# All ten key and value tiles of a transformer block summed by quarters, the context loaded and multiplied ahead of q, and the w_ada chunks in another order

## The chip, the cores and the metric

The kernel is one layer of a diffusion transformer on the 8 cores of one Trainium2 chip. The program is the same on each core, and no core talks to another: a core takes 1,024 of the 8,192 tokens (two samples of 4,096), a halo of 128 tokens on either side for the windowed keys, and its sample's 256 context tokens. The metric is the device time of the slowest core, in microseconds (us). Each core has a matrix engine (TensorE, PE in the profile), a vector engine (VectorE, DVE), ScalarE (ACT), GpSimd (POOL, used here only to issue loads) and SyncE (SP, issues the small loads, x and the stores).

## What is computed

```
m      = silu(c) @ w_ada + b_ada              # 6 x 2048 per sample: shift, scale, gate (mixer), shift, scale, gate (MLP)
h      = x * (1 + scale) + shift              # m[0], m[1]; the context has its own m from c_ctx
q,k,v,u,g = split(h @ w_in)                   # 1024, 256, 256, 1024, 1024 columns
k_ctx, v_ctx = (h_ctx @ w_in)[:, 1024:1536]
attn   = softmax over 384 window keys (axial rope on q, k), 256 context keys and a sink; 8 q heads, 2 kv heads
gmlp   = gelu(u) * (w_s @ LN(gelu(g)) + b_s)  # chunks of 128 positions
x      = LN(ALPHA * x + gate * ([attn, gmlp] @ w_out))
x      = LN(ALPHA * x + gate2 * (relu((x * (1 + scale2) + shift2) @ w_ff1) ** 2 @ w_ff2))
```

## The kernel before

The program is written as one list of operations. `P.add` notes what each reads and writes, and puts it at the end of its engine's list; a wait is set for each overlap with an earlier operation of another engine. So every engine runs its operations strictly in the order in which the code names them, and the code's order is the schedule. Loads stand in the list of POOL (weights, xT, context, rope tables, masks) or of SP (bias rows, x_tm, LayerNorm rows), and the list waits at a load whose target isn't free yet. Weights come in slots W0 to W3 of 16 KB per partition; `wload` takes the slot whose last use is the earliest, and loads 2,048 KB (bf16, read as 4 MB of fp32). PSUM has 8 banks, `PSB[0]` to `PSB[7]` (`psd` in the profile is 0 to 3, `ps` is 4 to 7); `bank()` takes the next of the list that `use_banks` has set.

The stages that the change touches:

- Start (L487 to L602). w_ada (2048 x 12288) is used in 24 chunks of 512 columns; chunk n of `ada_chunk` (L434) is 16 matmuls, a copy to `MT` (L449), and at the next `ada_flush` either four tiny matmuls and an addition into a column table `MODCOL` (chunks 0 to 7 and 12 to 19; L417, L423) or, for a gate (chunks 8 to 11, 20 to 23), one matmul and an addition into `GATE` (L409, L412). Chunks 0 to 7 are shift and scale of the mixer, and h needs them. For each quarter q of the 2,048 rows, four tiles of xT are loaded into `XTR`, chunks 4+q and q are computed, four tiles `HT` of h are formed (ACT even, VectorE odd), and key/value tiles 0 to 5 (128 tokens by 512 columns) are advanced by 4 matmuls each in banks 0 to 5 (L483). Tiles 6 to 9 are done whole behind it, 16 matmuls each (`kv_mm`, L340). `kv_evac` applies rope to k (four VectorE operations, L467 to L475) and copies v (L534); `kv_tr` transposes k. The context is loaded into `CTXT` over `XTR6` and `XTR7`, so only after the last tiles of h; 16 ACT operations form `HCT`, and `ctx_k`, `ctx_v` multiply it. Between them stand two tiles of q with the weight `Wq0`, and `bb_half`, which adds the row sums of w_s to the bias `BB` (L589).
- Attention loop (L685 to L770). 32 steps of scores, exp, transposes and products with v are laid beside 14 groups of q (steps with `qphase`), 16 of u and the first of g. `q_ada` and `u_ada` name the steps that carry a w_ada chunk.
- g stage and output projection (L834 to L945). 16 groups of g; `g_mix(t)` is the gating product of tile t (L799) with its VectorE chain (L804, L808); `g_ada` names the groups behind which a chunk stands. Then `wout_group(W, n, t)`: 16 matmuls, three VectorE operations (L824, L825, L814), the second of which needs tile t of x from `x_tm`. The x tiles 0 to 4 lie over `HT` and are loaded when the last g group is done. The groups of n = 0 stand in the order t = 5, 0, 6, 1, 7, 2, 3, 4.

Behind that come LayerNorm, the MLP in four passes and the last LayerNorm, which take 920 us and which the change leaves as they are.

## Time and profile before

| | |
|---|---|
| median of 3 runs | 1521.34 us (1520.41 to 1590.14) |
| profiled execution | 1515.89 us |
| its span, slowest core (core 4) | 1514.3 us |
| spans of the 8 cores | 1502.5 to 1514.3 us |
| TensorE busy | 1356.9 us, 90% |
| VectorE, ScalarE, GpSimd busy | 666.4, 341.8, 50.2 us |
| mean granted clock of TensorE | 0.961 |
| moved by DMA | 179.93 MB, 119 GB/s over the span |

Times in rows are microseconds from the start of the span of core 4, unless marked ns. The granted clock is a share of 2.4 GHz; 0.5 is 1.2 GHz. A row of the timeline is a run of like instructions of one engine: start, duration, and, in brackets, how long the engine had been idle and what it waited for.

### The profile page before, as it was taken

The page shows a single profiled execution, that of the slowest core. Times are in us where ns is not written, and L with a number is a line of the kernel's source. Part 1 is how long each engine was busy: PE and PEld are TensorE (multiplying, and loading weights), DVE is VectorE, ACT ScalarE, POOL GpSimd, SP SyncE. Part 2 cuts the span into 40 slices and gives each one's busy share as a digit, 9 for nine tenths or more (in the row PEclk, how much of TensorE's full clock was granted, in tenths as well). Part 3 has the DMA queues.
Part 4 walks back from the last instruction along what each step waited for, and adds up shares of the span by engine and source line. Part 5 has one row for each costly group of instructions (what it writes and reads, how often), then busy time and mean ns, then how long its engine had stood idle before and what let it go on. Part 6 is the DMA issues. An engine that isn't in the chain of part 4 may idle for free.

```text
span 1514.3 us, 19786 instructions; the slowest of 8 cores (1502.5 to 1514.3 us)
## 1 busy us (share of the span) xinstructions
PE 1356.9 (90%) x7289; PEld 660.1 (44%) x7430; DVE 666.4 (44%) x1215; ACT 341.8 (23%) x603; POOL 50.2 (3%) x94
## 2 busy tenths in 40 slices
PE   0343889999898999999999999999999999999995
PEld 0121455566444444444444444444444444444442
DVE  0010567788577567662344222443222333112677
ACT  0000256656553005521000111000111000111232
POOL 2010100000000000000000000000000000000000
PEclk9855899999999999999999999999999999999998
DMA  9999998667668994489542432523424425339312
GB/s 180 202 200 204 212 167 146 111 119 133 126 133 161 247 163 84 98 139 173 99 90 56 90 78 56 111 57 70 98 56 84 83 56 104 63 64 157 115 77 91
DMA packets 22687, 179.93 MB, mean 119 GB/s; under 512 B 3200, under 2 KB 7552, under 8 KB 11968
## 3 DMA queue, kind: packets, MB, share of 16 engines
q0 software_dynamic: 15328, 155.42, 55.8%
q1 hardware_dynamic: 7264, 23.23, 4.4%
q8 instruction: 61, 1.00, 0.3%
q14 instruction: 34, 0.28, 0.1%
HBM read 311.26 MB, written 8.39 MB: 211 GB/s over the span
## 4 chain that ended last, share of the span: by engine, by line
PE 75%; DMA 12%; DVE 4%; issue 4%; ACT 3%; another core or an unknown queue 2%; POOL 0%; DVEq 0%; ACTq 0%; SPq 0%; POOLq 0%
PE psd L340 31%; PE ps L340 30%; PE ps L483 6%; DMA regW<-w_in 3%; DMA regW<-w_ada 3%; DMA regW<-w_ff 2%; DMA regA<-x_tm 2%; PE ps L348 2%; DMA regB<-ctxT 2%; ACT regD L329 1%; PE ps L443 1%; DVE regD L625 1%; PE ps L666 1%; ACT regC L329 1%
## 5 line engine op out<-in xcount | busy, mean ns | idle before, releaser
L340 PE MATMUL ps<-regC,regW 128*128 128x512 bf16 (+1 forms) x1048 | 234.4, 378 | 6.0 <-ACT regC L329 3.3
L340 PE MATMUL psd<-regC,regW 128*128 128x512 bf16 x1052 | 237.0, 379 | 1.0
L329 ACT ACTIVATE regD<-ps 128x512 f32<-128x512 f32 (+1 forms) x91 | 57.0, 626 | 521.3 <-PE ps L340 511.4
L340 PEld LDWEIGHTS ps<-regC,regW 128*128 128x128 bf16 x1072 | 104.7, 98 | 130.6 <-issue 8.4
L340 PEld LDWEIGHTS psd<-regC,regW 128*128 128x128 bf16 x1072 | 104.6, 98 | 127.6 <-issue 1.6
L969 DVE TENSOR_TENSOR regW<-regD 128x512 bf16<-128x512 f32 x64 | 44.3, 693 | 179.7 <-ACT regD L329 179.7
L340 PE MATMUL ps<-regW 128*128 128x512 bf16 x504 | 120.2, 379 | 0.4
L340 PE MATMUL ps<-regW,regB 128*128 128x512 bf16 x502 | 120.1, 379 | 0.5
L340 PE MATMUL psd<-regW,regB 128*128 128x512 bf16 x439 | 104.9, 379 | 2.1 <-DMA regW<-w_ff 1.6
L340 PE MATMUL psd<-regW 128*128 128x512 bf16 x437 | 104.8, 379 | 0.6
L969 DVE TENSOR_TENSOR regB<-regD 128x512 bf16<-128x512 f32 x48 | 33.2, 693 | 132.5 <-ACT regD L329 132.5
L981 DVE TENSOR_TENSOR regD<-psd,regD 128x512 f32<-128x512 f32 x64 | 44.2, 691 | 103.7 <-PE psd L340 103.7
L981 DVE TENSOR_TENSOR regD<-ps,regD 128x512 f32<-128x512 f32 x64 | 44.2, 690 | 101.8 <-PE ps L340 101.8
L443 PE MATMUL ps<-regW,regC 128*32 128x512 bf16 x128 | 14.9, 616 | 81.9 <-DMA regW<-w_ada 81.9
L483 PE MATMUL ps<-regW,regA 128*128 128x512 bf16 x319 | 78.9, 388 | 1.0 <-issue 0.2
L329 ACT ACTIVATE regD<-psd 128x512 f32<-128x512 f32 x63 | 37.6, 597 | 175.3 <-PE psd L340 175.3
L340 PEld LDWEIGHTS ps<-regW,regB 128*128 128x128 bf16 x512 | 50.0, 98 | 60.5
L340 PEld LDWEIGHTS ps<-regW 128*128 128x128 bf16 x512 | 50.0, 98 | 60.5
L986 DVE TENSOR_TENSOR regA<-regA,regD 128x512 f32<-128x512 f32 x96 | 66.5, 692 | 10.0
L340 PEld LDWEIGHTS psd<-regW,regB 128*128 128x128 bf16 x448 | 43.7, 98 | 54.8 <-issue 2.1
L340 PEld LDWEIGHTS psd<-regW 128*128 128x128 bf16 x448 | 43.7, 98 | 53.0
L340 PE MATMUL psd<-regW,regC 128*128 128x512 bf16 x281 | 64.9, 385 | 0.4
(157 smaller groups left out, 1477.8 us busy)
## 6 DMA issues: line engine op xcount, KB each, us to landing
regW<-w_ff POOLq DMA_DIRECT2D x31, 2048.0 KB, 14.3
regW<-w_ada POOLq DMA_DIRECT2D x24, 2048.0 KB, 25.5
regW<-w_in POOLq DMA_DIRECT2D x7, 2048.0 KB, 18.9
regA<-x_tm SPq DMA_DIRECT2D x8, 1024.0 KB, 27.7
regW<-w_out POOLq DMA_DIRECT2D x4, 2048.0 KB, 18.5
regC<-xT POOLq DMA_DIRECT2D x12, 640.0 KB, 34.7
y<-regA SPq DMA_DIRECT2D x7, 1024.0 KB, 4.0
regB<-xT POOLq DMA_DIRECT2D x4, 640.0 KB, 42.5
```

The source lines that it names most:

```text
L329: return e.activation(out=out_ap, in_=in_ap, func=func, **kw)
L340: ins = te.matmul(ps_ap, lhsT=l, rhs=r, start=(i == 0), stop=(i == n - 1))
L348: ins = te.transpose(o_, i_, IDB.ap)
L443: ins = te.matmul(pb.ap[32 * g:32 * g + 32, :], lhsT=lhs.ap[:, k, :], rhs=W.ap[:, k, :], start=(i == 0), stop=(i == 3), tile_position=(0, ...
L483: ins = te.matmul(ps_ap, lhsT=l, rhs=r, start=(first and i == 0), stop=(last and i == n - 1))
L625: vec(lambda e, a=a, ps=ps: e.tensor_reduce(out=MX[r].ap[:, a:a + 1], in_=ps.ap[:, 0:640], axis=AX.X, op=ALU.max), [ps], [MX[r]])
L666: ins = te.matmul(po.ap[:, a * 128:(a + 1) * 128], lhsT=pts[a].ap[:, j * 128:(j + 1) * 128], rhs=vv, start=(j == 0), stop=(j == 4))
L969: vec(lambda e: e.tensor_tensor(out=hk_.ap, in0=rl.ap, in1=rl.ap, op=ALU.mult), [rl], [hk_])
L981: vec(lambda e: e.tensor_tensor(out=tmp.ap, in0=pb.ap, in1=GATE[n].ap, op=ALU.mult), [pb, GATE[n]], [tmp])
L986: vec(lambda e: e.tensor_tensor(out=xb.ap, in0=xb.ap, in1=tmp.ap, op=ALU.add), [xb, tmp], [xb])
```

## The change

The four key/value tiles 6 to 9 are now also advanced by quarters: for q = 0, 1, 2 each gets 4 matmuls in bank 6, and the result is copied (q = 0, ACT) or added (q = 1, 2, VectorE) to a sum `KVS` in SBUF; `kv_mm` does only the last quarter, and `kv_evac` adds it to the sum. The w_ada chunks of the start use bank 7 alone, and take their 16 rows in another order. v is copied by ACT. The context goes to three places that nothing holds at the time (`CT`: over `GATE`, behind `XTR7`, and over the context's keys and values), so its three loads stand ahead of rope and `Wq0`, and wait for nothing; the bias rows of `GATE` are loaded behind its use. The products of the context stand ahead of the two q tiles. `bb_half` moves to the u groups 3 and 7. The q steps carry chunks 12 to 14 (columns), the u steps 8 to 11 (gates), chunk 17 stands one g group earlier, and the banks of the output groups from (0, 2) on have another order.

```diff
-        CTXT = mk("CTXT", "B", 0, F32, [16, CTX])
...
+        KVS = [mk("KVS%d" % t, "D", PM[0].lo + t * 2048, F32, [512]) for t in range(4)]
...
+        CT = [mk("CT%d" % k, "D", GATE[0].lo + k * 1024, F32, [CTX]) for k in range(8)]
+        CT += [mk("CT%d" % (8 + k), "B", 10240 + k * 1024, F32, [CTX]) for k in range(6)]
+        CT += [mk("CT%d" % (14 + k), "A", 51200 + k * 1024, F32, [CTX]) for k in range(2)]
...
-                        k = 4 * g + i
+                        k = 4 * i + g
...
-        use_banks([6, 7])
+        use_banks([7])
...
+            for t in range(NKP, NH):
+                if q == 3:
+                    break
+                pb, kvs = PSB[6], KVS[t - NKP]
+                mm_part(pb.ap, [(HT[k].ap[:, t * 128:(t + 1) * 128], Wkv.ap[:, k, :]) for k in range(4 * q, 4 * q + 4)],
+                        [Wkv] + HT[4 * q:4 * q + 4], pb, True, True)
+                if q == 0:
+                    act(kvs.ap, pb.ap, AF.Copy, [pb], [kvs])
+                else:
+                    vec(lambda e, kvs=kvs, pb=pb: e.tensor_tensor(out=kvs.ap, in0=pb.ap, in1=kvs.ap, op=ALU.add), [pb, kvs], [kvs])
+        for k0, k1 in ((0, 8), (8, 14), (14, 16)):
+            c0 = CT[k0]
+            dst = tiles[c0.region][:, c0.lo // 4:c0.lo // 4 + (k1 - k0) * CTX].rearrange("p (k t) -> p k t", t=CTX)
+            dma("gpsimd", dst, ctxT[k0 * 128:k1 * 128, :].rearrange("(k p) t -> p k t", p=128), "ctx%d" % k0, "slot", writes=CT[k0:k1])
         cload(ROPEC, ropeC.rearrange("(t p) d -> p t d", p=128), "gpsimd", grp="r")
         cload(ROPES, ropeS.rearrange("(t p) d -> p t d", p=128), "gpsimd", grp="r")
         Wq0 = wload("win", 0)
-        dma("gpsimd", CTXT.ap, ctxT.rearrange("(k p) t -> p k t", p=128), "ctx", "slot", writes=[CTXT])
...
+        for k in range(16):
+            act(HCT[k].ap, CT[k].ap, AF.Identity, [CT[k], MODCOL[0], MODCOL[1]], [HCT[k]],
+                bias=MODCOL[0].ap[:, k, 1:2], scale=MODCOL[1].ap[:, k, 1:2])
         gate_bias(2)
...
-            mm_group(pb.ap, [(HT[k].ap[:, t * 128:(t + 1) * 128], Wkv.ap[:, k, :]) for k in range(16)], [Wkv] + HT, [pb])
+            mm_part(pb.ap, [(HT[k].ap[:, t * 128:(t + 1) * 128], Wkv.ap[:, k, :]) for k in range(12, 16)],
+                    [Wkv] + HT[12:16], pb, True, True)
...
-            rope(pb, 0, 2, t, KR[t % 3])
-            vec(lambda e: e.tensor_copy(out=Vb[t].ap, in_=pb.ap[:, 256:512]), [pb], [Vb[t]])
+            src = pb
+            if t >= NKP:
+                src = KVS[t - NKP]
+                vec(lambda e: e.tensor_tensor(out=src.ap, in0=pb.ap, in1=src.ap, op=ALU.add), [pb, src], [src])
+            rope(src, 0, 2, t, KR[t % 3])
+            act(Vb[t].ap, src.ap[:, 256:512], AF.Copy, [src], [Vb[t]])
...
-        q_ada = {(0, 4): 8, (1, 0): 9, (1, 4): 10}
+        q_ada = {(0, 4): 12, (1, 0): 13, (1, 4): 14}
...
-        u_ada = {1: 11, 5: 12, 9: 13, 13: 14}
+        u_ada = {1: 8, 5: 9, 9: 10, 13: 11}
...
+                        elif gi in (3, 7):
+                            bb_half(gi // 4, mains[(gi + 1) % 2])
...
-        g_ada = {6: 15, 10: 16, 14: 17}
+        g_ada = {6: 15, 10: 16, 13: 17}
...
-        use_banks([2, 3, 6, 7, 0, 1, 4, 5])
+        use_banks([7, 4, 5, 0, 1, 2, 3, 6])
```

TensorE at the start, from the last quarter's matmuls (L483) on: L340 with 512 columns is a key/value or q tile, with 256 columns a context product, L348 a transpose. Before:

```order
L483 MATMUL ps<-regW,regA 128x512 x4
L340 MATMUL ps<-regW,regA 128x512 x32
L348 MATMUL psd<-regD,regC 128x128 x4
L340 MATMUL psd<-regW,regA 128x512 x16
L348 MATMUL psd<-regD,regC 128x128 x4
L340 MATMUL psd<-regW,regA 128x512 x16
L348 MATMUL ps<-regD,regC 128x128 x4
L340 MATMUL psd<-regW,regA 128x512 x16
L348 MATMUL ps<-regD,regC 128x128 x4
L340 MATMUL psd<-regW,regA 128x512 x16
L340 MATMUL ps<-regC,regW 128x256 x16
```

And TensorE at the same place now (L487, L344 and L352 are the same helpers; the first row holds tiles 6 and 7's last quarter too):

```order
L487 MATMUL ps<-regW,regA 128x512 x12
L352 MATMUL psd<-regD,regC 128x128 x4
L487 MATMUL psd<-regW,regA 128x512 x4
L352 MATMUL psd<-regD,regC 128x128 x2
L487 MATMUL psd<-regW,regA 128x512 x4
L352 MATMUL psd<-regD,regC 128x128 x2
L344 MATMUL psd<-regC,regW 128x256 x16
L352 MATMUL ps<-regD,regC 128x128 x2
L344 MATMUL psd<-regC,regW 128x256 x16
L352 MATMUL ps<-regD,regC 128x128 x2
L344 MATMUL ps<-regW,regC 128x256 x16
```

The four whole tiles are gone from here, and the context products stand where they were; the two q tiles come behind them.

POOL's list of loads behind the last w_ada chunk of the eight. Before:

```order
L317 DMA regA<-ropeS 128x10x128
L317 DMA regW<-w_in 128x8192
L317 DMA regB<-ctxT 128x16x256
L317 DMA regD<-w_sT 128x1024
L317 DMA regA<-masks 128x768
L317 DMA regD<-b_s 128x1024
L317 DMA regW<-w_ada 128x8192
```

And POOL's list at that place now:

```order
L321 DMA regB<-ctxT 128x6x256
L321 DMA regA<-ctxT 128x2x256
L321 DMA regA<-ropeC 128x10x128
L321 DMA regA<-ropeS 128x10x128
L321 DMA regW<-w_in 128x8192
L321 DMA regD<-w_sT 128x1024
L321 DMA regA<-masks 128x768
```

The context moved from behind the q weight (w_in) to ahead of the rope tables.

TensorE in the output projection, with the numbers of banks and slots (psd0 is banks 0 and 1, psd1 is 2 and 3; regC is the input, regW1 and regW0 the weights of n = 0 and 1; L799 is the gating product). Before:

```order
L799 MATMUL ps5<-regD,regB 128x128 x4
L340 MATMUL psd1<-regW1,regC 128x512 x32
L340 MATMUL ps6<-regW1,regC 128x512 x16
L340 MATMUL psd1<-regW1,regC 128x512 x32
L340 MATMUL ps6<-regW1,regC 128x512 x16
L340 MATMUL ps7<-regW0,regC 128x512 x16
L340 MATMUL psd0<-regW0,regC 128x512 x32
L340 MATMUL ps4<-regW0,regC 128x512 x16
L443 MATMUL ps5<-regW2,regD 32x512 x16
```

And TensorE there now:

```order
L819 MATMUL ps5<-regD,regB 128x128 x4
L344 MATMUL psd1<-regW1,regC 128x512 x32
L344 MATMUL ps6<-regW1,regC 128x512 x16
L344 MATMUL ps7<-regW1,regC 128x512 x16
L344 MATMUL ps4<-regW1,regC 128x512 x16
L344 MATMUL ps5<-regW1,regC 128x512 x16
L344 MATMUL psd0<-regW0,regC 128x512 x32
L344 MATMUL psd1<-regW0,regC 128x512 x32
L447 MATMUL ps6<-regW2,regD 32x512 x16
```

The three groups behind t = 7 had banks 2, 3 and 6, and now have 7, 4 and 5.

## Rows read from the trace of the kernel before

**Rows 1.** The page: TensorE over the span, DMA in 40 slices (tenths).
```profile
PE 1356.9 (90%) x7289; PEld 660.1 (44%) x7430; DVE 666.4 (44%) x1215; ACT 341.8 (23%) x603; POOL 50.2 (3%) x94
DMA  9999998667668994489542432523424425339312
```

**Rows 2.** Chain of waits, 150 to 205 us: start, duration, what.
```profile
109.73 43.24 DMA regW<-w_ada
...
161.72 22.75 DMA regB<-ctxT
...
192.67 3.27 PE ps L340 x16
...
202.05 1.73 PE ps L483 x8
```

**Rows 3.** Timeline of TensorE, 105 to 235 us.
```profile
107.28 1.90 PE L443 MATMUL ps<-regW,regC 128*32 128x512 bf16 x16 [4.60 <-DMA regW<-w_ada]
...
167.49 7.07 PE L340 MATMUL ps<-regW,regA 128*128 128x512 bf16 x31
...
215.60 1.05 PE L443 MATMUL ps<-regW,regD 128*32 128x512 bf16 x16
```

**Rows 4.** Timeline of POOL: when three of the loads were issued.
```profile
111.51 0.97 POOL L317 DMA_DIRECT2D regA<-ropeS  x1
122.41 0.56 POOL L317 DMA_DIRECT2D regW<-w_in  x1 [9.93 <-PE ps L443]
...
164.47 0.58 POOL L317 DMA_DIRECT2D regW<-w_ada  x1
```

**Rows 5.** DMA view, one issue each (ropeS, W_q, w_ada): us to landing.
```profile
regA<-ropeS POOLq DMA_DIRECT2D x1, 640.0 KB, 51.1
...
regW<-w_in POOLq DMA_DIRECT2D x1, 2048.0 KB, 54.9
...
regW<-w_ada POOLq DMA_DIRECT2D x1, 2048.0 KB, 44.0
```

**Rows 6.** Timeline of VectorE: a key/value tile, a q rope, bb_half, a u step.
```profile
167.61 0.42 DVE L467 TENSOR_TENSOR regC<-psd,regA 128x256 f32<-128x256 f32 x1
...
169.06 0.42 DVE L534 CAST regA<-psd 128x256 bf16<-128x256 f32 x1
...
190.12 0.69 DVE L467 TENSOR_TENSOR regC<-psd,regA 128x512 f32<-128x512 f32 x1 [0.55 <-PE psd L340]
...
191.77 0.69 DVE L475 TENSOR_TENSOR regC<-regC 128x512 bf16<-128x512 f32 x1
...
198.65 3.54 DVE L589 SCALAR_TENSOR_TENSOR regD<-psd,regD 128x128 f32<-128x128 f32 x8 [6.19 <-PE psd L340]
...
316.48 0.29 DVE L682 COPY regC<-ps 128x256 bf16<-128x256 bf16 x1 [0.24 <-PE ps L348]
...
322.00 0.29 DVE L682 COPY regC<-ps 128x256 bf16<-128x256 bf16 x1 [0.31 <-PE ps L348]
```

**Rows 7.** Timeline of TensorE, 465 to 526 us.
```profile
469.99 1.84 PE L417 MATMUL ps<-regD 128*128 128x2 f32 x8 [4.28 <-DVE regD L449]
...
501.94 8.75 PE L340 MATMUL ps<-regW,regC 128*128 128x512 bf16 x32 [3.23 <-DVE regB L824]
...
525.43 0.95 PE L417 MATMUL psd<-regD 128*128 128x2 f32 x8
```

**Rows 8.** Timeline of VectorE: the second and the fifth tile of x arrive.
```profile
499.71 0.69 DVE L825 SCALAR_TENSOR_TENSOR regA<-regA,regB 128x512 f32<-128x512 f32 x1 [8.28 <-DMA regA<-x_tm]
...
509.26 0.69 DVE L825 SCALAR_TENSOR_TENSOR regA<-regA,regB 128x512 f32<-128x512 f32 x1 [0.92 <-DMA regA<-x_tm]
```

**Rows 9.** SP issues x, POOL a w_ada chunk, and its time to landing.
```profile
465.80 0.87 SPq L317 DMA_DIRECT2D regA<-x_tm  x2
...
466.25 0.53 POOL L317 DMA_DIRECT2D regW<-w_ada  x1 [3.02 <-PE psd L340]
...
regW<-w_ada POOLq DMA_DIRECT2D x1, 2048.0 KB, 32.7
```

More of the change, by code:

```diff
@@ L583, in ctx_v, with bb_half @@
             act(VC.ap[:, tb, :], pb.ap[:, 0:256], AF.Copy, [pb], [VC])
-        def bb_half(i):
-            pb = PSB[2 + i]
+        def bb_half(i, pb):
             mm_group(pb.ap, [(ONESB.ap, WST.ap[:, 4 * i:4 * i + 4, :].rearrange("p a b -> p (a b)"))], [ONESB, WST], [pb])
```

68 lines of the change are left out of this document (32 added, 36 removed).

## The prediction, made before the changed kernel ran

> **What bounds the kernel now.** I read the page first: TensorE is busy for 1356.9 of 1514.3 us, and the DMA engines are full in the first slices [rows 1]. So the change can act only where TensorE waits: behind the loads at the start, and in the few gaps later. The chain of waits for 150 to 205 us shows how the start ends: the last w_ada chunk of the eight lands at 153.0, the context load is issued at 161.72 and takes 22.75 us (it lands at 184.5), sixteen ACT operations follow, the first context product starts at 192.67, and the first attention step at 202.05 [rows 2]. The TensorE timeline shows that this stretch is full apart from that wait: it ran four whole key/value tiles and two q tiles before the context products [rows 3]. The POOL rows and the landings behind them show one queue served in order: ropeS (issued 111.51) landed 51.1 us later at 162.6, W_q (issued 122.41) 54.9 later at 177.3, then the context at 184.5 and the next w_ada chunk (issued 164.47) 44.0 later at 208.5 [rows 4, 5]. With the engines full, a load issued earlier only swaps places.
>
> The second place is the start of the output projection. TensorE waits 4.28 us for the copy of chunk 17, runs the next matmuls at half clock (1.84 us for what took 0.95 at 525.43), then waits 3.23 us for a PSUM bank, and again runs at half clock (32 matmuls in 8.75 us) [rows 7]. The bank was held because VectorE waited 8.28 us for the second tile of x [rows 8].
>
> **The start, part by part.** (a) Side sums: for q = 0, 1, 2 four more 4-matmul pieces go to one bank, each followed by one ACT or VectorE operation. 31 such matmuls take 7.07 us at full clock [rows 3], so four take 0.9 us, and twice that at half clock; with 0.69 us for a 512-wide VectorE operation [rows 6] and two hand-overs of 0.1 a piece costs 1.8 to 2.7 us, and the last of four ends 6.3 to 9.9 us behind the first's start. Before, TensorE had only 4.60 us there in q = 1, until 107.28 [rows 3]. So chunk 6's product and the slot that it frees come up to 5 us late, but the load behind it waits over 40 us in the queue anyway (43.24) [rows 2]. I cost it at nothing; the cover is that queue. After 167.5 the four tiles need 16 matmuls and not 64: 3.45 us in place of 13.8 (0.86 for four).
>
> (b) The context goes ahead of rope and W_q. In the queue it took 184.5 - 177.3 = 7.2 us. So it lands at 160.3, rope at 169.8, W_q at 184.5, since the sum ahead of W_q is what was ahead of the context [rows 4, 5]. The 16 ACT operations run at 161 to 169, beside the loads. VectorE starts on rope at 169.8 rather than 165.7; a tile costs it 1.45 us [rows 6], V's copy going to ACT, and the last four tiles 0.6 more. Nine tiles end near 184.6, when W_q lands, so both are late at once.
>
> (c) What is late next is W_q: q tile 0 runs 184.5 to 188.1, its rope (2.3 us, [rows 6]) to 190.5, the tenth tile to 192.6, its transposes to 192.9, and the first attention step starts at 193.1 in place of 201.9: 8.8 us sooner. Two things take from it. The step with a w_ada product stood at 215.60, 13.7 us behind the first; it would be at 206.8, but its chunk still lands at 208.5 [rows 3, 5]. That leaves 215.6 - 208.5 = 7.1. And after gaps of 2.7 us and more the rows show half clock (16 matmuls of 256 columns in 3.27 us [rows 2], where half of 3.45 is due); I take 0.5 for it. **Start: -6.6 us**, with -9 (no such wait) and -3 (half clock over both q tiles, 3.5 more) as ends.
>
> **The attention loop.** Three gate chunks move from the q steps to the u steps, three column chunks the other way; both flushes cost TensorE about 0.9 us, so this is nothing. bb_half, eight VectorE operations of 3.54 us in all, stood ahead of the first scores, where VectorE was idle for 6.19 us. Now four of them stand in each of u steps 3 and 7. In plain u steps (5.5 us apart) VectorE idles only 0.24 to 0.31 us at a time [rows 6]. So each costs 1.8 less 0.3, twice: 3.0, and 0.2 for its matmul. **Loop: +3.2 us**; 1 if the scores' lead absorbs it, 4.5 if the gap slows the clock.
>
> **The output projection.** Chunk 17 one group earlier takes its copy out of the way: the first output group then waits only for its gating product (469.6 in place of 472.5), the next two for theirs as well. The new bank order gives (0,2), (0,3), (0,4) the banks 7, 4, 5, all free, in place of 2, 3, 6. TensorE then ends (0,4) at about 499.0; before it was at about 507.5. Alone, this is worth 8.6 us at the next hand-over.
>
> But two things hang on (0,4). It frees the slot of W_out 0, so W_out 2 is issued 8.5 us earlier. And the x tiles are still in flight: they are issued at 465.8 to 468 on SP; the second lands at 499.7, as the w_ada load does (466.25 + 32.7 = 499.0), the fifth at 509.26 [rows 8, 9]. Two tiles of 1.05 MB in 33.9 us beside the weights is 62 GB/s; three more in the 9.6 us without them is 328 GB/s. In the changed kernel W_out 1 is issued 3.8 us earlier (its slot is freed by chunk 17), so the weights end 3.8 us sooner and x could be done at 506. W_out 2, issued at 499.3 and moving from about 501.3, cuts into that: at 3.2 us a tile, 1.5 tiles (1.5 MB) are left then. At 62 GB/s they take 25 us, and the fifth tile lands at 526; that pace includes the start of the first tile, so I take 75 GB/s, 20 us, and 521.5.
>
> Then VectorE is late: its queue holds (0,4), (1,0) to (1,3), at 2.2 us each (three operations of 0.69 and gaps), then chunk 18's copy: 521.5 + 1.5 + 8.8 + 0.7 = 532.5. TensorE waits for this copy with the product that stood at 525.43 without a wait [rows 7]; queued behind it is all that TensorE has. With half clock after the wait (1.84 for 0.95, and 1.5 in the next group) the loss is 7.1 - 0.3 + 2.4 = 9.2 us. If the tile lands at 514 the hand-over is on time, and the loss 1 to 2; at 526 it is 14. I take 6, between 514 and 521.5 and nearer to the second, since the rows of the second tile and of the w_ada chunk are the nearest there are. **Output projection: +6 us**, ends -8.6 and +14.
>
> The Trainium skill, "DMA: Bandwidth & Descriptors", section Queues, rings and completion order, says that each DMA engine serves the rows it has work for in turn, a packet at a time. As an estimate by that rule, with 8 KB of x to 16 KB of weight per turn at 328 and 168 GB/s, x gets 67 GB/s; the rows say 62, so the trace agrees, and the fifth tile would land at 524 rather than 526. The rule speaks against issuing W_out 2 earlier: a second queue doesn't shield x.
>
> **The sum.** -6.6 + 3.2 + 6 = +2.6 us on 1515.89, the profiled execution (its span is 1514.3): 1518.5. The median of the runs is 1521.34, 5.4 us above that execution, so the median goes to **1524 us**.
>
> **Rivals.**
> A. *The x tail doesn't bite* (25%). If W_out 2 is slower to start than I think, or x is through by then, VectorE is not late and the 8.6 us stay. Then -6.6 + 3.2 - 8.6 = -12: 1509. For it speaks that x would be through at 506, 7 us behind W_out 2's issue; against it that weights held x at 62 GB/s for 34 us.
> B. *Slower, by one mechanism: chunk 19 follows W_out 2 without a gap* (12%). It is issued when chunk 18's product is done (about 514), before W_out 2 has landed; if x gets under 50 GB/s the tail runs into it, and tile five lands at 530 and more. Each microsecond of delay behind 514 is one of TensorE; at 530 the stage costs +18, the sum +14 to +15: 1536. Over 2% would need tile five at 546, which nothing in the rows gives.
> C. *The start's gain is larger or whole, the rest neutral* (10%): the chunk isn't late, the tail lands at 514: -9 + 3.2 + 1.5 = -4: 1517.
> D. *The side sums reach the path* (5%). In q = 2 they end near 146 and chunk 7's products near 151; chunk 3 lands at 153.1. With 3.3 us a piece and not 2.7 they would push chunk 3's product: +1 to +3 at the start, 1526.
> My forecast, a change of -2 to +8 us, has 48%.
>
> **Chances.** The range that leaves out 2 in 10 reaches from A to most of B: 1508 to 1534; the likeliest case alone is 1519 to 1529. All cases lie within 2% (30 us, about what a measurement of this kernel tells from no change): within 2% 0.97, faster 0.01, slower 0.02.
>
> **What would show it.** Right: the context lands near 160, W_q near 184, the first attention step starts near 193; the w_ada product of the third step waits one or two us for its DMA; u steps 3 and 7 are 1.5 us longer than their neighbours; no wait for a bank at the fourth output group; VectorE waits for x_tm with the fifth tile, and the flush of chunk 18 waits for the copy on VectorE by some 10 us. Wrong: W_q landing before 180 (the queue isn't served in order); TensorE waiting in the first 150 us for side sums; the fifth x tile landing by 510 of the old time (rival A); or q tiles at half clock.

## The result, and the profile after

The changed kernel takes 1506.61 us (median of 20 runs, 1503.8 to 1751.32), the kernel before beside it 1517.65 (median of 20). The ratio is **0.9939, interval 0.9924 to 0.9954**: 9.3 us faster (7.0 to 11.5), within 2%. Forecast were 2.6 us slower and 1524 us in a range of 1508 to 1534. The direction was wrong, and the median lies just below the range. Part of the miss in microseconds is the kernel before itself, which was 3.7 us faster here than the 1521.34 that the forecast started from; the ratio on that number would be 1512. (A few executions of either kernel are disturbed and over 1.5% longer; the ratios leave them out.) The profiled execution took 1506.71 us; its slowest core is core 7. First its page, TensorE over the span and DMA in 40 slices (of before in [rows 1]), then the spans of three cores:

```profile
PE 1361.0 (90%) x7430; PEld 656.2 (44%) x7430; DVE 671.8 (45%) x1217; ACT 347.4 (23%) x617; POOL 51.5 (3%) x96
DMA  9999998757669994499523424425335234249212
```

```profile
core 0: 1497.0 us, clock 0.967
...
core 4: 1499.2 us, clock 0.971
...
core 7: 1505.1 us, clock 0.970
```

Busy time says nothing here: TensorE is busy for 4 us more, and the kernel ends 9 us sooner. (The trace before also lacks the records of 141 matmuls: 7289 beside 7430 weight loads.) What does tell is how far apart the w_ada products stand, since each ends a stage. The table gives the differences of their starts in the timelines, as median over the eight cores with the range in brackets where it is over 1 us.

| from the product of | to | before | after | difference | forecast |
|---|---|---|---|---|---|
| last start chunk (3) | first q-step chunk | 60.6 (59.2-62.5) | 51.6 (49.1-55.3) | -9.0 | -6.6 |
| first q-step chunk | chunk at u 1 | 83.3 | 83.1 | -0.2 | 0 |
| chunk at u 1 | at u 9 | 47.8 | 52.1 | +4.3 | +3.2 |
| chunk at u 9 | 16 | 95.7 (94.0-97.4) | 95.7 (94.1-97.4) | 0.0 | 0 |
| 16 | 18 | 74.0 (72.0-76.9) | 69.8 | -4.2 | +6 |
| 18 | 23 | 185.5 (184.7-186.5) | 185.2 (184.7-186.5) | -0.3 | 0 |

The sum is -9.4; the last start chunk's own product stands at 152.6 before and 152.8 after in the medians (150.8 to 152.7 in the eight other kernels with the side sums, 151.5 in the one without). The row from u 9 to 16 moves in steps: the stretch from u 13 to chunk 15 takes 52.0 or 53.7 us on different cores of one run, and the next one some 18.1 or 19.8; why, no run shows. So three stages carry the result, and the output projection alone is 10.2 us off the forecast.

**The start.** Landings on core 7: ropeS was issued at 116.08, W_q at 124.67 and the next w_ada chunk at 145.86; the DMA view gives the time of each to landing (answers to [rows 4, 5]):

```profile
116.08 0.96 POOL L321 DMA_DIRECT2D regA<-ropeS  x1
124.67 0.56 POOL L321 DMA_DIRECT2D regW<-w_in  x1 [7.64 <-PE ps L447]
...
145.86 0.53 POOL L321 DMA_DIRECT2D regW<-w_ada  x1 [19.01 <-PE ps L447]
...
regA<-ropeS POOLq DMA_DIRECT2D x1, 640.0 KB, 55.1
...
regW<-w_in POOLq DMA_DIRECT2D x1, 2048.0 KB, 57.7
...
regW<-w_ada POOLq DMA_DIRECT2D x1, 2048.0 KB, 55.2
```

So they landed at 171.2, 182.4 and 201.1 (forecast 169.8, 184.5, 208.5). VectorE's timeline from there (189.72 is the rope of q tile 0, 196.15 the end of that of q tile 1), and TensorE's first attention step and w_ada product (answers to [rows 2, 3, 6]):

```profile
171.26 0.42 DVE L471 TENSOR_TENSOR regC<-psd,regA 128x256 f32<-128x256 f32 x1 [10.22 <-DMA regA<-ropeS]
...
173.05 0.42 DVE L471 TENSOR_TENSOR regC<-psd,regA 128x256 f32<-128x256 f32 x1
...
183.66 0.68 DVE L557 TENSOR_TENSOR regD<-ps,regD 128x512 f32<-128x512 f32 x1
...
185.99 0.68 DVE L557 TENSOR_TENSOR regD<-psd,regD 128x512 f32<-128x512 f32 x1
...
189.72 0.69 DVE L471 TENSOR_TENSOR regC<-psd,regA 128x512 f32<-128x512 f32 x1 [1.32 <-PE ps L352]
...
196.15 0.69 DVE L479 TENSOR_TENSOR regC<-regC 128x512 bf16<-128x512 f32 x1
```

```profile
194.88 1.89 PE L487 MATMUL ps<-regW,regA 128*128 128x512 bf16 x8
...
208.59 1.05 PE L447 MATMUL ps<-regW,regD 128*32 128x512 bf16 x16
```

VectorE works from 171.26 to 196.84, with one wait of over 1 us: a tile costs it 1.79 us (171.26 to 173.05) and 2.33 with a side sum to add (183.66 to 185.99). That one wait, 1.32 us at 189.72, is for q tile 0 from TensorE, which had run without a wait from 174.85 on; every core has it (1.2 to 2.0 us). So up to q tile 0 it is TensorE that ends last, with VectorE close behind, and from there VectorE with two tiles. W_q is never waited for (it landed 1.2 to 3.6 us ahead of q tile 0 on the eight cores), nor is the w_ada chunk, which has been there for 7.5 us at 208.59. The landing of ropeS sets when this chain begins: on the eight cores the first q-step product stands 37.2 to 38.1 us behind it, while that landing itself varies by 5.4 us against the last start chunk's product.

**The output projection.** TensorE, VectorE with x, and the issues, core 7 (answers to [rows 7 to 9]):

```profile
461.19 0.95 PE L421 MATMUL ps<-regD 128*128 128x2 f32 x8
...
464.67 0.38 PE L819 MATMUL ps<-regD,regB 128*128 128x128 bf16 x4 [2.23 <-DVE regB L824]
465.47 8.62 PE L344 MATMUL psd<-regW,regC 128*128 128x512 bf16 x32 [0.41 <-DVE regD L427]
...
481.49 13.97 PE L344 MATMUL ps<-regW,regC 128*128 128x512 bf16 x64
495.30 13.98 PE L344 MATMUL psd<-regW,regC 128*128 128x512 bf16 x64
...
513.65 0.95 PE L421 MATMUL ps<-regD 128*128 128x2 f32 x8
```

```profile
461.44 2.49 SPq L321 DMA_DIRECT2D regA<-x_tm  x5
...
454.45 0.53 POOL L321 DMA_DIRECT2D regW<-w_out  x1 [12.89 <-PE ps L447]
461.90 0.53 POOL L321 DMA_DIRECT2D regW<-w_ada  x1 [6.91 <-PE psd L344]
496.00 0.53 POOL L321 DMA_DIRECT2D regW<-w_out  x1 [33.57 <-PE ps L344]
...
489.87 0.69 DVE L845 SCALAR_TENSOR_TENSOR regA<-regA,regB 128x512 f32<-128x512 f32 x1 [3.54 <-DMA regA<-x_tm]
499.51 0.69 DVE L845 SCALAR_TENSOR_TENSOR regA<-regA,regB 128x512 f32<-128x512 f32 x1 [0.95 <-DMA regA<-x_tm]
```

The wait for the copy of chunk 17 is gone (461.19 has none), and so is the wait for a bank. VectorE has the fifth tile of x at 499.51, 38.1 us behind the issue of x, and the flush of chunk 18 at 513.65 waits for nothing. Forecast was a wait there of some 10 us for VectorE's copy. W_out 2 was issued at 496.00, but it had not begun to move: the DMA view of 496.1 to 499.7 has no line for POOL's queue (q0), only SP's:

```profile
q1 hardware_dynamic: 163, 1.20, 98.0%
```

In the trace the first packet of W_out 2 comes 3.8 to 4.4 us behind its issue on the eight cores (38.4 to 38.9 us behind the issue of x), and the fifth tile of x has landed by then on all of them (36.9 to 38.7).

### The profile page after: what moved, and what is told of

It reads as the page before. It is cut to its first block, busy times and chain, and to the rows that moved or that the text cites. A ratio compares the mean times of both kernels' runs of the same rounds, so it can differ in the third digit from the quotient of the medians.

```text
span 1505.1 us, 19966 instructions; the slowest of 8 cores (1495.7 to 1505.1 us)
## 1 busy us (share of the span) xinstructions
PE 1361.0 (90%) x7430; PEld 656.2 (44%) x7430; DVE 671.8 (45%) x1217; ACT 347.4 (23%) x617; POOL 51.5 (3%) x96
## 4 chain that ended last, share of the span: by engine, by line
PE 75%; DMA 8%; DVE 7%; issue 5%; ACT 3%; another core or an unknown queue 2%; DVEq 0%; POOL 0%; ACTq 0%; POOLq 0%
PE psd L344 32%; PE ps L344 28%; PE ps L487 7%; DMA regW<-w_ada 5%; DMA regW<-w_ff 2%; ACT regD L333 2%; PE ps L352 2%; PE ps L447 1%; DVE regA L1030 1%; PE psd L487 1%; DVE regD L643 1%; DVE regB L824 1%; PE ps L684 1%; DVE regD L1001 1%
## 5 line engine op out<-in xcount | busy, mean ns | idle before, releaser
L344 PE MATMUL psd<-regC,regW 128*128 128x512 bf16 (+1 forms) x1104 | 238.9, 376 | 1.3 <-DMA regW<-w_ff 1.3
L344 PE MATMUL ps<-regC,regW 128*128 128x512 bf16 x1040 | 228.4, 379 | 0.6 <-ACT regC L333 0.6
L344 PEld LDWEIGHTS psd<-regC,regW 128*128 128x128 bf16 x1104 | 107.7, 98 | 129.0 <-issue 3.4
L344 PEld LDWEIGHTS ps<-regC,regW 128*128 128x128 bf16 x1040 | 101.5, 98 | 124.8 <-issue 3.5
L344 PE MATMUL psd<-regW,regB 128*128 128x512 bf16 x480 | 115.0, 383 | 2.1 <-DMA regW<-w_ff 2.1
L344 PE MATMUL ps<-regW,regB 128*128 128x512 bf16 x480 | 113.4, 379 | 0.0
L344 PE MATMUL ps<-regW 128*128 128x512 bf16 x480 | 113.4, 379 | 0.0
L344 PE MATMUL psd<-regW 128*128 128x512 bf16 x480 | 113.4, 379 | 0.0
L487 PE MATMUL ps<-regW,regA 128*128 128x512 bf16 x392 | 94.5, 384 | 8.4 <-DVE regD L526 5.9
L333 ACT ACTIVATE regD<-psd 128x512 f32<-128x512 f32 x65 | 38.8, 597 | 183.2 <-PE psd L344 183.2
L344 PEld LDWEIGHTS psd<-regW,regB 128*128 128x128 bf16 x480 | 47.2, 99 | 59.9 <-issue 4.3
L344 PEld LDWEIGHTS psd<-regW 128*128 128x128 bf16 x480 | 47.0, 98 | 56.9 <-issue 0.6
L344 PEld LDWEIGHTS ps<-regW 128*128 128x128 bf16 x480 | 47.0, 98 | 56.6
L344 PEld LDWEIGHTS ps<-regW,regB 128*128 128x128 bf16 x480 | 46.9, 98 | 56.7
L344 PE MATMUL psd<-regW,regC 128*128 128x512 bf16 x304 | 68.3, 385 | 1.6 <-ACT regC L333 1.2
## 6 DMA issues: line engine op xcount, KB each, us to landing
regW<-w_out POOLq DMA_DIRECT2D x4, 2048.0 KB, 18.1
```

The source lines that it names most:

```text
L333: return e.activation(out=out_ap, in_=in_ap, func=func, **kw)
L344: ins = te.matmul(ps_ap, lhsT=l, rhs=r, start=(i == 0), stop=(i == n - 1))
L487: ins = te.matmul(ps_ap, lhsT=l, rhs=r, start=(first and i == 0), stop=(last and i == n - 1))
```

## Experiments on the output projection

Which of the two edits gave the 4.2 us, and was the danger to x real? The two edits are chunk 17's place (14 or 13) and the order of the banks (old or new).

**The new banks alone**, on the kernel before:

```diff
-        use_banks([2, 3, 6, 7, 0, 1, 4, 5])
+        use_banks([7, 4, 5, 0, 1, 2, 3, 6])
```

> The kernel before with the new order of banks for the output groups alone. Theory 1: TensorE reaches group (0, 4) without the wait for a bank (3.2 us and 1.9 us of half clock on core 4, less on others), W_out 2 is issued about 5 us earlier while 1 to 1.5 tiles of x are still to come, the fifth tile lands 5 to 15 us later than before, and the kernel is 3 to 10 us slower. Theory 2 (no contention to speak of): 3 to 5 us faster.

Ratio 0.9995 (0.9982 to 1.0008), between the two theories and in the range of neither. The stage took 72.2 us (71.8 to 72.6), 1.8 less; but from chunk 18 to 19, which is 29.5 us elsewhere, three cores took 32.9, 42.7 and 37.1. Core 4, VectorE's waits for x and TensorE behind them:

```profile
499.06 0.69 DVE L825 SCALAR_TENSOR_TENSOR regA<-regA,regB 128x512 f32<-128x512 f32 x1 [0.61 <-DMA regA<-x_tm]
511.87 0.69 DVE L825 SCALAR_TENSOR_TENSOR regA<-regA,regB 128x512 f32<-128x512 f32 x1 [10.73 <-DMA regA<-x_tm]
...
522.83 1.84 PE L417 MATMUL ps<-regD 128*128 128x2 f32 x8 [9.49 <-DVE regD L449]
```

This is the forecast's chain, link by link: x cut short by W_out 2 (issued 37.2 us behind x), VectorE 10.73 us late, the copy of the w_ada product behind it, TensorE waiting 9.49 us and then at half clock (1.84 for 0.95). Here W_out 1 is issued 3.1 us ahead of x, as in the kernel before.

**The changed kernel with chunk 17 back in its place:**

```diff
-        g_ada = {6: 15, 10: 16, 13: 17}
+        g_ada = {6: 15, 10: 16, 14: 17}
```

> The changed kernel with chunk 17 back at g group 14. Theory 1 (chunk 17's place is what gets x through in time: it issues W_out 1 about 4 us earlier, into an idle DMA queue): W_out 1 comes later against x, the last x tile falls into W_out 2 on some cores, which then wait for the copy of chunk 18 by 3 to 10 us, as three cores do with the banks alone; with the first wait (4.3 in place of 2.2 and half clock) the stage is 2 to 3 us longer on all cores, and the kernel 3 to 9 us slower than the changed one. Theory 2 (the place only moves a copy out of the way): 2 to 3 us slower, no core waits for chunk 18's copy.

Ratio 0.9932 (0.9895 to 0.9969) beside 0.9939: no difference that the runs can tell, where either theory had 2 us and more. In the profile the stage is 72.1 us in place of 69.8, and chunk 18 to 19 has 30.6 to 33.6 on three cores (waits for the copy of 0.8 to 2.2 us). So x was late here too, but by little: less than was expected.

**Chunk 17's place alone**, on the kernel before:

```diff
-        g_ada = {6: 15, 10: 16, 14: 17}
+        g_ada = {6: 15, 10: 16, 13: 17}
```

> The kernel before with chunk 17 one g group earlier, and nothing else. With b_banks, a_g14 and the changed kernel this fills the table of chunk place by bank order, for the stretch from chunk 16's product to chunk 18's: 74.0 (14, old), 72.2 (14, new), 72.1 (14, new, changed kernel), 69.8 (13, new, changed kernel). Theory: the place takes away the wait for the copy (4.28 us) and lets W_out 1 run 4 us earlier, so that x lands 3 to 5 us sooner and the old banks come free in time: 70 to 71.5 on all cores, and the spread of 72.0 to 76.9 over the cores shrinks to under 1.5 us. Rival: with the old order VectorE, which still waits for the second x tile, holds the bank as before, and the stage stays at 72 to 75.

Ratio 0.9976 (0.9964 to 0.9988). The stage took 70.8 us (69.4 to 72.2), so the spread didn't shrink to 1.5, and chunk 19 was never late. The wait for the old bank is still there on two cores (2.38 and 1.08 us, for VectorE L824), so the rival was right in part. (On the chip that ran this kernel, cores 4 to 7 took 1.6 us more here in other kernels too, 71.3 to 71.6 against 69.5 to 69.8; this kernel's cores 0 to 3 alone have a median of 69.9.) The table is now full: 74.0 (14, old), 72.2 (14, new), 69.9 to 70.8 (13, old), 69.8 (13, new). Chunk 17's place is worth 2.3 to 4.1 us, the banks up to 1.8 and little of it behind the other edit; and the place is also what keeps x out of the way of W_out 2: with it W_out 1 is issued 7.0 us ahead of x and not 3.1 us, and the two weight loads are through 25.2 to 27.9 us behind the issue of x in the changed kernel, against 29.1 to 33.1 before.

**x made late on purpose:** the LayerNorm row (1 MB, to all partitions) is loaded ahead of x and not behind it.

```diff
+        dma("sync", LN1G.ap, ln1_g.partition_broadcast(128), "ln1p", "group", writes=[LN1G])
         for t in range(5):
             load_xt(t)
         use_banks([7, 4, 5, 0, 1, 2, 3, 6])
-        dma("sync", LN1G.ap, ln1_g.partition_broadcast(128), "ln1p", "group", writes=[LN1G])
```

> The changed kernel with one LayerNorm row load (1 MB) ahead of the x tiles on SP. Theory 1 (x and W_out 2 do contend as forecast, but x was through just in time): the fifth x tile lands at 50 to 53 us behind the issue of the first and not at 38, the copy of chunk 18 comes at 61 to 64 and TensorE waits for it for 9 to 11 us; the kernel is 9 to 12 us slower than the changed one. Theory 2 (weights on the other queue hardly slow x, the forecast's price was wrong): the fifth tile lands at 41 to 42, TensorE waits for nothing, 0 to 1 us.

Ratio 1.0000 (0.9978 to 1.0023): the whole gain of the change is gone. Core 0, VectorE with the fifth tile and TensorE with the flush of chunk 18:

```profile
510.68 0.69 DVE L845 SCALAR_TENSOR_TENSOR regA<-regA,regB 128x512 f32<-128x512 f32 x1 [10.59 <-DMA regA<-x_tm]
...
521.64 1.84 PE L421 MATMUL ps<-regD 128*128 128x2 f32 x8 [9.98 <-DVE regD L453]
```

Chunk 18 to 19 took 29.5 to 48.5 us, median 36.1 in place of 29.5. 1 MB more ahead, which is 3 us where x has the engines to itself, cost 1.7 to 19 us on six cores, since what is left of x when W_out 2 comes moves at a fraction of its pace: in the kernel before, x had 61 GB/s beside weights (470 to 480 us on core 4, 0.61 MB) and 339 without them (503 to 508, 1.70 MB). The fifth tile landed 40.9 to 56.6 us behind the issue of the first, where theory 1 had 50 to 53. The forecast's mechanism holds; its place in time did not.

## Experiments on the attention loop

**bb_half's products one by one in eight q steps**, in place of two u steps:

```diff
+        def bb_one(h, pb):
+            mm_group(pb.ap[:, 0:128], [(ONESB.ap, WST.ap[:, h, :])], [ONESB, WST], [pb])
+            vec(lambda e: e.scalar_tensor_tensor(out=BB.ap[:, h * 128:(h + 1) * 128], in0=pb.ap[:, 0:128], scalar=BCOL.ap[:, h:h + 1],
+                in1=BB.ap[:, h * 128:(h + 1) * 128], op0=ALU.mult, op1=ALU.add), [pb, BCOL, BB], [BB])
...
+                    if t in (2, 3, 6, 7):
+                        bb_one(4 * c + (t - 2 if t < 4 else t - 4), mains[(t + 1) % 2])
...
-                        elif gi in (3, 7):
-                            bb_half(gi // 4, mains[(gi + 1) % 2])
```

> The changed kernel with bb_half taken out of u groups 3 and 7 and given head by head (one 128-column matmul, one VectorE operation of about 0.45 us) to eight q steps without a w_ada chunk. Theory 1 (VectorE has no room in a u step, and the whole +4.4 us between the w_ada products of the u steps is bb_half's): that stretch shortens by 4.4 us, the q steps stay as they are, and the kernel is 4 to 4.5 us below the changed one. Theory 2 (the four gate chunks that moved to the u steps cost it): nothing changes, within 1 us.

Ratio 0.9914 (0.9898 to 0.9931), median 1501.65. The stretches u 1 to 5 and 5 to 9 are back at 23.9 us (26.0 and 26.1 in the changed kernel), with the gate chunks still in them, so those cost nothing; the q steps stay at 51.6 on six cores and take 52.1 and 53.2 on two.

**bb_half at the end of the start**, as in the kernel before:

```diff
         rope(PSB[3], 0, 4, 2, QR[1])
         kv_tr(9)
+        bb_half(0, PSB[4])
+        bb_half(1, PSB[7])
```

> The changed kernel with bb_half at the end of the start, ahead of the first attention step, as in the kernel before. Theory 1: the u steps lose the 4.4 us again, and the first scores' reduction waits for 3.6 us of VectorE work, so the sum is -1 us (between -2 and +1). Theory 2 (gate chunks cost the 4.4 us): +3.6 us.

Ratio 0.9919 (0.9905 to 0.9932). The loop is back at 23.9 us, and the start is 54.0 in place of 51.6. The eight operations now cost 2.4 us at the start, behind the last VectorE work of its chain, against 4.3 in the u steps and about nothing in the q steps. The stages say -1.9 us against the changed kernel, the ratio -3; theory 1 had -1. In the changed kernel, core 7, the u step that holds the first half shows this (VectorE's four operations, and TensorE waiting for them):

```profile
333.32 1.72 DVE L583 SCALAR_TENSOR_TENSOR regD<-ps,regD 128x128 f32<-128x128 f32 x4
...
335.19 1.89 PE L487 MATMUL ps<-regA,regW 128*128 128x512 bf16 x8 [1.56 <-DVE regD L583]
```

## Experiments on the start

**No side sums:** tiles 6 to 9 are multiplied whole behind the last quarter, as before; the context stays ahead.

```diff
-            for t in range(NKP, NH):
-                if q == 3:
-                    break
-                pb, kvs = PSB[6], KVS[t - NKP]
...
-            mm_part(pb.ap, [(HT[k].ap[:, t * 128:(t + 1) * 128], Wkv.ap[:, k, :]) for k in range(12, 16)],
-                    [Wkv] + HT[12:16], pb, True, True)
+            mm_part(pb.ap, [(HT[k].ap[:, t * 128:(t + 1) * 128], Wkv.ap[:, k, :]) for k in range(16)],
+                    [Wkv] + HT, pb, True, True)
```

> The changed kernel without the side sums: tiles 6 to 9 whole again, 16 matmuls each, ahead of the context products. Theory: 48 more matmuls are 10.3 us of TensorE, of which the 7 us that TensorE stood idle between 169.9 and 186 in the changed kernel cover most; the third q step's w_ada product comes at 54 to 57 us behind the last product of the start in place of 51.6, so +3 to +5 us. If the side sums were worth nothing (the queue alone binds): 0 to +1.

Ratio 0.9964 (0.9933 to 0.9995). The start takes 58.8 us (57.9 to 59.5; expected were 54 to 57), however much the landing of ropeS varies: TensorE is the bound, and does not wait for loads. Core 1, the whole tiles one behind the other:

```profile
164.50 7.93 PE L487 MATMUL ps<-regW,regA 128*128 128x512 bf16 x36
...
173.17 3.61 PE L487 MATMUL psd<-regW,regA 128*128 128x512 bf16 x16 [0.51 <-ACT regA L333]
```

So with the context ahead the side sums are worth 7.2 us in the median core's start, of the 10.4 of matmuls that they take away. The whole kernel, whose time is that of its slowest core, loses less by the ratio: 3.8 us, with the intervals just touching (0.9964 against 0.9939). The slowest start is 59.5 in place of 55.3, 4.2 us more.

**The context back behind W_q**, side sums kept:

```diff
+        cload(ROPEC, ropeC.rearrange("(t p) d -> p t d", p=128), "gpsimd", grp="r")
+        cload(ROPES, ropeS.rearrange("(t p) d -> p t d", p=128), "gpsimd", grp="r")
+        Wq0 = wload("win", 0)
         for k0, k1 in ((0, 8), (8, 14), (14, 16)):
...
-        cload(ROPEC, ropeC.rearrange("(t p) d -> p t d", p=128), "gpsimd", grp="r")
-        cload(ROPES, ropeS.rearrange("(t p) d -> p t d", p=128), "gpsimd", grp="r")
-        Wq0 = wload("win", 0)
```

> The changed kernel with the three context loads behind W_q in POOL's list, still waiting for nothing. Theory 1 (the queue got 6 us quicker because the context's 1 KB rows no longer run beside the bias rows of GATE): the context lands at 172 to 178, the w_ada chunk of the third q step about 53 us behind the last chunk of the start, as before, and that product stands 55 to 58 us behind the last product of the start (51.6 in the changed kernel, 60.6 before). Theory 2 (it is the early issue, not the order): the chunk lands 47 us behind, as in the changed kernel, and the start is limited by the 16 ACT operations behind the context, 54 to 56 us.

Ratio 1.0020 (0.9990 to 1.0051): no faster than the kernel before. The start takes 66.8 us (63.5 to 76.1), 15.2 more than in the changed kernel and outside both theories; the w_ada chunk landed 49.0 us behind the last start chunk (45.0 to 58.9), between the two. The run doesn't decide between them: the bias rows were issued behind the context here, at 171.6 us and later, and not beside it. Core 1, where ACT's list holds the context operations ahead of the copies of v and k, and TensorE waits for the first of these:

```profile
173.74 4.04 ACT L333 ACTIVATE regC<-regD 128x256 bf16<-128x256 f32 x8 [13.87 <-DMA regD<-ctxT]
...
182.12 0.64 PE L352 MATMUL psd<-regD,regC 128*128 128x128 bf16 x4 [14.82 <-ACT regA L333]
```

In the changed kernel each edit needs the other: without the side sums TensorE is the bound (58.8), and without the early context ACT is held (66.8). How much of the 66.8 is due to ACT's list, where the context operations now stand ahead of all copies, isn't shown: the side sums on the kernel before, with its own order on ACT, were not run. The context alone brought little because the kernel before hardly waited for it: ACT waited for its landing 0.8 to 1.7 us on four cores, and not at all on the other four.

**Why the queue ran faster than the sum ahead said.** From the landing of the last start chunk to that of the next w_ada chunk took 51.5 to 55.5 us before and 43.6 to 51.5 after, medians 53.5 and 46.9, with the same loads to bring, part of them moved ahead. SP's queue has four b_ada loads (1 MB in all) in this stretch, issued at 163 to 165 us on core 4 before and at 165 to 167 on core 7 after. Their time to landing, and what POOL's queue (q0) and SP's (q1) moved meanwhile (packets, MB, share of the engines), core 4 before from 176 to 184 us and core 7 after from 188 to 200:

```profile
regD<-b_ada SPq DMA_DIRECT2D x4, 256.0 KB, 22.7
...
q0 software_dynamic: 378, 1.29, 74.5%
q1 hardware_dynamic: 336, 0.56, 27.9%
```

```profile
regD<-b_ada SPq DMA_DIRECT2D x4, 256.0 KB, 40.2
...
q0 software_dynamic: 145, 2.08, 94.3%
q1 hardware_dynamic: 144, 0.26, 6.8%
```

Before, b_ada moved mostly beside the context and small loads and took one byte for 2.3 of POOL's; after, mostly beside the w_ada chunks behind them, and took one for 8.

To see what they cost, they were moved behind the start, in either kernel:

```diff
-        gate_bias(2)
...
         vec(lambda e: e.tensor_scalar(out=NSINK8.ap, in0=SINK8.ap, scalar1=-1.0, scalar2=None, op0=ALU.mult), [SINK8], [NSINK8])
+        gate_bias(2, after=[NSINK8])
```

Kernel before with this edit:

> The kernel before, with only the four loads of b_ada (1 MB, issued by SyncE at 163 us, landed some 21 us later) moved behind the last rope of the start. Theory: in the kernel before they share the DMA engines with the context, the masks and b_s (the context took 11.8 to 12.9 us behind W_q on seven cores, b_s 6 us), and in the changed kernel with W_q, where they get less of each turn and land 40 us after issue; that is why its POOL queue ended 6 us sooner. By it the context lands 2.5 to 3.5 us sooner here, the start (last w_ada product of the eight to the first of the q steps) goes from 60.6 to 57 to 58.5 us, and the whole to 0.998. Rival: the queue of before is slow because the context and the loads behind it are issued only at 161 us; then the landings stay where they are and the start at 60 to 61. The ten q-step chunks may wait a little for the gate's bias, which comes later.

Ratio 0.9991 (0.9975 to 1.0008). The landings moved as the theory said: the context came 7.0 to 11.6 us behind W_q (median 9.1; before 7.2 to 13.4, median 11.9), b_s 3 us behind the masks (6 before), and the w_ada chunk 46.7 us behind the last start chunk, 6.8 sooner (5.8 against the other kernel that ran on this chip with its b_ada in place). The start did not move: 60.4 us, where 57 to 58.5 were expected. Core 1 had its context at 178.5 (161.29 + 17.2), began its context operations at 183.42, behind a copy of transposed keys, and had the first attention step at 199.38:

```profile
regB<-ctxT POOLq DMA_DIRECT2D x1, 2048.0 KB, 17.2
...
regW<-w_ada POOLq DMA_DIRECT2D x1, 2048.0 KB, 32.5
```

```profile
182.66 0.86 ACT L329 ACTIVATE regA<-ps 128x256 bf16<-128x256 bf16 x2 [2.82 <-PE ps L348]
183.42 7.96 ACT L329 ACTIVATE regC<-regB,regD 128x256 bf16<-128x256 f32 x16
...
191.52 1.91 PE L340 MATMUL ps<-regC,regW 128*128 128x256 bf16 x16 [1.77 <-ACT regC L329]
...
199.38 1.89 PE L483 MATMUL ps<-regW,regA 128*128 128x512 bf16 x8
```

The context is 4.6 us earlier than in the kernel before on this core, and nothing uses it: ACT's list reaches it only behind that copy, which waits 2.82 us for TensorE's transposes, and these stand behind the whole tiles.

Changed kernel with this edit:

> The changed kernel with the same four loads of b_ada behind the start. Its start ends 37.4 us behind the landing of ropeS on every core. b_ada is issued at 162 to 165 us, when ropeS is nearly there. Theory (b_ada shares turns with what is in flight): ropeS lands at most 1 us sooner, W_q and w_ada 1 to 2 us sooner, and the start stays within 1 us of 51.6, since it waits for neither. Rival (b_ada costs its full 3.2 us wherever it stands): ropeS up to 3 us sooner and a start near 49.

Ratio 0.9935 (0.9914 to 0.9956), start 51.5 us, the w_ada chunk 46.1 us behind the last start chunk (46.9 without the edit). So b_ada had cost this kernel's queue one microsecond at most (the other kernels with an early context and all their b_ada in place have 45.5 to 47.7), and that of the kernel before six to seven. Why it cost more there than the 3.2 us that 1 MB takes at full pace is open; the two queues together moved 234 GB/s from 176 to 184 us.

**Two tries at a shorter start.** The rope tables ahead of the context, with bb_half in the q steps:

```diff
+        cload(ROPEC, ropeC.rearrange("(t p) d -> p t d", p=128), "gpsimd", grp="r")
+        cload(ROPES, ropeS.rearrange("(t p) d -> p t d", p=128), "gpsimd", grp="r")
         for k0, k1 in ((0, 8), (8, 14), (14, 16)):
...
-        cload(ROPEC, ropeC.rearrange("(t p) d -> p t d", p=128), "gpsimd", grp="r")
-        cload(ROPES, ropeS.rearrange("(t p) d -> p t d", p=128), "gpsimd", grp="r")
```

> The kernel with bb_half spread over the q steps, and the two rope loads ahead of the context's. Theory: VectorE's chain of ten tiles starts at about 166 and not 171, TensorE is through with the context products when W_q lands (about 180), and the start is 2 to 4 us shorter: 47 to 49 us to the third q step's product, where the chunk's own landing (47 behind) binds. The context lands 7 us later, 167 to 170; its 16 ACT operations then hold back the copies of v and of the first transposes; if that binds, 0 to +3 us.

Ratio 0.9916 (0.9873 to 0.9959), as with the bb edit alone (0.9914). ropeS landed at 154.9 to 162.8, some 9 us sooner, and the start took 50.9 us all the same (50.3 to 57.1; 50.7 with the bb edit alone), where 47 to 49 were expected. VectorE, which could begin sooner, now waits 1.2 to 4.4 us for q tile 0: TensorE's work behind the first transposes is what takes the time. TensorE itself waits 0.5 to 5.2 us for ACT at these transposes (median 1.6); core 1, the slowest start, has the most:

```profile
174.04 0.64 PE L352 MATMUL psd<-regD,regC 128*128 128x128 bf16 x4 [5.15 <-ACT regA L333]
```

**All of it, and the context operations of ACT in fours** behind the first four key/value tiles, b_ada behind the start:

```diff
         kv_mm(6, PSB[6])
         kv_evac(0)
+        for k in range(0, 4):
+            act(HCT[k].ap, CT[k].ap, AF.Identity, [CT[k], MODCOL[0], MODCOL[1]], [HCT[k]],
+                bias=MODCOL[0].ap[:, k, 1:2], scale=MODCOL[1].ap[:, k, 1:2])
```

> The changed kernel with bb_half's eight products one by one in the q steps, the rope tables ahead of the context, the sixteen context operations of ACT in fours behind the first four key/value tiles, and b_ada behind the start. In the run with rope first TensorE waited for ACT, whose list held all context operations ahead of the first copy of v, and the start stayed at 50.9. Theory: with that wait gone the start is bound by VectorE from the end of the last key/value tile on (about 163, 2 us before ropeS landed at 165) or by W_q: 46 to 49 us where the w_ada chunk has landed, so 2 to 4 us less than the run with single bb products (0.9914): 0.988 to 0.990. Rival: the w_ada chunk, which lands 43 to 51 us behind the last of the start, now ends last: start 48 to 51, ratio 0.990 to 0.992.

Ratio 0.9925 (0.9907 to 0.9944), start 54.1 us (53.7 to 55.0): worse by 3 us than with ACT's list in one piece, and the theory fell. The start is now nearly the same on all cores, so it no longer hangs on loads. TensorE waits three times for ACT, 3.4 to 4.7 us in all, as its transposes and their copies stand behind four context operations each. Core 1 has the most:

```profile
171.67 1.02 PE L487 MATMUL psd<-regW,regA 128*128 128x512 bf16 x4 [1.96 <-ACT regA L333]
...
176.67 1.91 PE L344 MATMUL psd<-regC,regW 128*128 128x256 bf16 x16 [1.36 <-ACT regA L333]
```

VectorE waits 5.1 to 6.4 us for q tile 0 here, so TensorE is the bound and not, as the theory had it, VectorE.

The fastest version measured is the changed kernel with bb_half's products in the q steps: 0.9914, some 4 us faster than the change.

## Why the prediction was wrong, step by step

**The output projection: forecast +6, measured -4.2. This step decided.** The step that failed is "W_out 2, issued at 499.3 and moving from about 501.3, cuts into that", with x done at 506: the overlap of x and W_out 2. Counted from the issue of x, the forecast had W_out 2 issued at 33.5 us, moving at 35.5, and x done at 40.2, so 4.7 us of x were left to be slowed. Measured in the medians were: W_out 2 issued at 34.6, its first packet at 38.8, and the fifth tile of x landed at 37.6. Nothing was left. Of the difference

- 2.2 us are the start of W_out 2: 4.2 us from issue to the first packet, where I had put 2 without a row for it. Weight loads that are issued with nothing else in flight have their first packet after 2.0 to 2.4 us (core 7, from 282 us on); beside SP's loads W_out 2 took nearly twice as long;
- 2.6 us are x, which landed sooner. I had taken 3.8 us off core 4's x, for the weights that end sooner, and core 4 was the slowest there: its weights were through 33.1 us behind the issue of x, those of the others 29.1 to 32.8. In the changed kernel they were through at 26.0 in the median (31.1 before), because W_out 1 was issued 7.0 us ahead of x and not 3.1;
- 1.1 us are the later issue of W_out 2.

The mechanism behind the +6 (a cut x, VectorE late, the w_ada copy behind it) is real: it ran on three cores with the new banks alone, and on six with x made late. The penalty is a cliff: where x is through as W_out 2 starts to move, it is nothing; with 3 us more ahead of x it was 1.7 to 19 us on six cores. I took a value from the middle of a range with such a cliff in it, 4.7 us from the edge. Rival A is what happened, and both reasons that it names came true (W_out 2 slower to start, x through by then); with 25% it had too little. The gain was smaller than its 8.6 us, for core 4's wait for a bank (3.23 us and half clock behind it) was not that of the others: the eight cores have 0 to 3.23 us there, median 1.5. Core 4 itself won 7.1.

**The start: forecast -6.6, measured -9.0.** The first attention step was to come 8.8 us sooner. Counted from the last start chunk's product it came 9.0 sooner in the medians (46.9 and 37.8), which is close; but on core 4, from which the forecast was made, it came at 189.0 and not at 193.1, 12.9 sooner. The agreement is partly luck, since the reason was another. I had W_q and VectorE late at the same time. W_q was never waited for, and up to q tile 0 TensorE ended last. VectorE's tile cost 1.65 to 1.79 us and not 1.45: tiles stood 1.79 apart in the kernel before too, v's copy included, so taking the copy out gave back 0.14 us at most. It also waits for its own results (0.17 to 0.24 us in the rows).

The term for a late w_ada chunk, 1.7 us (208.5 against 206.8), failed outright: "its chunk still lands at 208.5" rested on the sum of bytes ahead in POOL's queue, and left out SP's. The chunk landed at 201.1 on core 7 and 198.5 on core 4. In the kernel before, 1 MB of b_ada shared the engines with the context, the masks and b_s; in the changed kernel it moved later, mostly beside the 16 KB packets of w_ada, and got so little that it landed twice as late.

The Trainium skill, "DMA: Bandwidth & Descriptors", section Queues, rings and completion order, says that a DMA engine serves the rings that have work a packet each in turn. The packets of this trace are 2 KB for b_ada, 4 KB for the context and 16 KB for the weights, so by that rule b_ada takes one byte for two of the context's and one for eight of w_ada's. The trace agrees: 0.56 MB beside 1.29 MB from 176 to 184 us before, 0.26 MB beside 2.08 MB from 188 to 200 after.

The half clock (+0.5) was there on some cores only: on core 7, behind the wait of 3.39 us for ropeS, eight matmuls ran at a granted clock of 0.54 and took some 1.6 us more, on core 3 likewise; five cores have none.

**The attention loop: forecast +3.2, measured +4.3.** The place and the mechanism were right (TensorE waits 1.56 us for L583); the term was 1.6 a step and measured 2.1 and 2.2. The four operations take 1.72 us, and the 0.3 us that I let the idle time absorb was not there; the other 0.4 us a step are not explained.

**Side sums in the first 150 us: nothing, as forecast.** A piece took 2.04 us on core 4 and the product of chunk 6 stood 2.7 us later in the medians, but no load behind it came later. Rival D didn't happen. Chunks moved between q and u steps: nothing, as forecast.

The sum of the forecast was made against core 4 of one execution. By that core alone the start won 11.9 us and the output 7.1. The median over the cores, which the table above uses, would have shown what was core 4's own.

## What to carry over

Read a term from all cores before it is used: where the slowest core of one profile has a wait, look whether the others have it, and how much of it. Where two queues run side by side, the sum of bytes ahead in one of them isn't enough; list what the other queue moves in the same stretch, and the size of its packets against the size of theirs. Give the time from a load's issue to its first packet a row of its own, from a stretch in which the other queue is as busy. And where a cost has a cliff (a transfer that is either through in time or crawls beside another), don't take the middle: say on which side of the edge it falls, what decides that, and give each side its chance.

## What the runs showed that was not expected

- A 1 MB load on another queue cost the queue beside it 6 to 7 us in one order (53.5 to 46.7 when it was taken away) and 1 us at most in another (46.9 to 46.1), though it was issued within some 2 us of the same time and moved the same bytes.
- In the changed kernel, which has the landing of ropeS on the path of its start, the rest repeats to a microsecond from there: 37.2 to 38.1 us behind ropeS on eight cores, while the landings spread over 5.4 us. Without side sums the relation is missing (57.9 to 59.5 us, with ropeS landing 12.3 to 19.2 us behind the last start chunk's product): the load is off the path. Even where it holds, the next bound can be close: with ropeS 9 us sooner the start gained nothing.
- Making a load's consumer wait less can cost more than it gives on an engine that runs in order: with the context operations in fours between the key/value tiles TensorE waited 3.4 to 4.7 us for ACT, with all sixteen ahead of them 1.6 us in the median (0.5 to 5.2), and the start was 3 us longer.
